# Four RMS norms of a two-layer hybrid block, taken in two halves of the positions beside the weight tiles around them

## The reference

```
for l in range(2):
    h  = rms_norm(x, ln1) * (1 + sc1) + sh1          # layer 0 and 1, 768 positions
    x  = x + g1 * merge(mixers(h @ w_in)) @ w_out
    h2 = rms_norm(x, ln2) * (1 + sc2) + sh2          # 768 positions in layer 0, 512 in layer 1
    x  = x + g2 * square(relu(h2 @ w_mlp1)) @ w_mlp2
return rms_norm(x, final_norm)                       # 512 positions
rms_norm(x, g) = x * rsqrt(mean(x*x over the 1024 channels) + 1e-6) * g
```

## Time and profile before

| | us |
|---|---|
| median of 3 runs | 2155.12 (2152.6 to 2156.09) |
| profiled execution, its own time | 2153.41 |
| its span, first to last instruction | 2151.5 |
| PE busy | 2101.2 (98%) |
| DVE / ACT / POOL busy | 1302.1 / 512.4 / 906.7 |

### The profile page before, as it was taken

How to read it: one execution, slowest core, us unless ns; L and a number is a source line. 1 busy time by engine, 2 the same in 40 slices (tenths; PEclk the granted TensorE clock), 3 DMA queues, 4 the chain that set the end, 5 groups by cost and what they waited for, 6 DMA issues and landing times.

```text
span 2151.5 us, 29928 instructions
## 1 busy us (share of the span) xinstructions
PE 2101.2 (98%) x12112; PEld 1885.5 (88%) x12112; DVE 1302.1 (61%) x1987; ACT 512.4 (24%) x818; POOL 906.7 (42%) x492
## 2 busy tenths in 40 slices
PE   6999999999999999999999999999999999999998
PEld 5999999867899899999999989888777787888886
DVE  6998991555663577576686643693266757263353
ACT  4115121454301230111201112312365213010010
POOL 2531442200244264444434443545511465766662
PEclk9999999999999999999999999999999999999999
DMA  7373355232552134435355326345310532322221
GB/s 286 105 154 101 111 180 155 101 121 101 223 179 79 40 127 144 138 137 177 127 172 169 134 95 189 118 178 170 130 34 24 213 114 70 112 92 95 98 98 69
DMA packets 107980, 277.20 MB, mean 129 GB/s; under 512 B 22938, under 2 KB 42778, under 8 KB 106062
## 3 DMA queue, kind: packets, MB, share of 16 engines
q1 hardware_dynamic: 71520, 200.31, 27.5%
q10 hardware_dynamic: 36334, 75.07, 10.6%
HBM read 237.00 MB, written 37.88 MB: 128 GB/s over the span
## 4 chain that ended last, share of the span: by engine, by line
PE 94%; DVE 3%; ACT 1%; DMA 1%; issue 0%; SPq 0%; POOL 0%; DVEq 0%; ACTq 0%; POOLq 0%
PE ps L497 72%; PE ps L506 3%; PE ps L1135 3%; PE ps L1009 2%; PE ps L1149 2%; PE ps L1185 2%; PE ps L512 1%; PE ps L1035 1%; PE ps L1047 1%; PE ps L614 1%; PE ps L1082 1%; PE ps L860 1%; PE ps L998 1%; DMA raw<-in_w_main 1%; PE ps L737 1%; PE ps L1050 0%
## 5 line engine op out<-in xcount | busy, mean ns | idle before, releaser
L1375 POOL TENSOR_SCALAR whi<-raw 128x1024 fp32r<-128x1024 f32 x244 | 273.6, 1121 | 1192.9 <-PE ps L497 660.7
L1378 POOL TENSOR_TENSOR wlo<-raw,whi 128x1024 fp32r<-128x1024 f32 x244 | 633.6, 2597 | 20.4
L497 PE MATMUL ps<-hh,whi 128*128 128x384 f32 (+1 forms) x1512 | 450.1, 353 | 0.3 <-ACT mr L1814 0.3
L497 PE MATMUL ps<-hl,whi 128*128 128x384 f32 (+1 forms) x1512 | 447.6, 351 | 0.0
L497 PE MATMUL ps<-hh,wlo 128*128 128x384 f32 (+1 forms) x1512 | 447.6, 351 | 0.0
L497 PEld LDWEIGHTS ps<-hh,whi 128*128 128x128 f32 x1512 | 275.3, 188 | 20.2 <-issue 1.1
L497 PEld LDWEIGHTS ps<-hl,whi 128*128 128x128 f32 x1512 | 276.4, 188 | 18.5 <-issue 0.2
L497 PEld LDWEIGHTS ps<-hh,wlo 128*128 128x128 f32 x1512 | 276.3, 188 | 18.6
L2237 DVE SCALAR_TENSOR_TENSOR x<-ps,ada,x 128x384 f32<-128x384 f32 (+1 forms) x160 | 80.4, 546 | 274.8 <-PE ps L497 274.8
L497 PE MATMUL ps<-midh,whi 128*128 128x384 f32 (+1 forms) x768 | 231.1, 354 | 1.8 <-DVE midl L2264 1.8
L497 PE MATMUL ps<-midh,wlo 128*128 128x384 f32 (+1 forms) x768 | 229.6, 353 | 0.0
(11 more groups left out here) (270 smaller groups left out, 3037.1 us busy)
## 6 DMA issues: line engine op xcount, KB each, us to landing
raw<-in_w_main SPq DMA_DIRECT2D x244, 512.0 KB, 3.3
dot_w<-in_ada_dot SPq DMA_DIRECT2D x64, 512.0 KB, 4.1
ada_mixer<-in_ada_w SPq DMA_DIRECT2D x32, 512.0 KB, 4.0
g_d<-gt ACTq DMA_DIRECT2D x24, 384.0 KB, 2.4
gl<-g_d ACTq DMA_DIRECT2D x8, 1152.0 KB, 5.4
ada_first<-in_ada_w SPq DMA_DIRECT2D x16, 512.0 KB, 14.8
cout_d<-cz SPq DMA_DIRECT2D x12, 512.0 KB, 4.9
cout<-cout_d ACTq DMA_DIRECT2D x6, 1024.0 KB, 8.5
```

The lines of the kernel that those rows point to most:

```text
L497: ins = pe.matmul(bank(p, h, a, b), ww[:, w % W_SLOTS, kw * P:(kw + 1) * P], xx[:, kx, a:b], start=(first and i == 0 and j == 0), stop=(la ...
L1375: pool.tensor_scalar(whi[:, u, :], raw[:, u % 2, :], 1.0, 0.0, ALU.mult, ALU.add).then_inc(w_split.sem, 1)
L1378: pool.tensor_tensor(wlo[:, u, :], raw[:, u % 2, :], whi[:, u, :].bitcast(F32), ALU.subtract).then_inc(w_split.sem, 1)
```

## The change

For norms A, B, C and D the last four tiles of the product ahead (`FULL = 4`) are taken half by half: first all four for the first half of the positions (h = 0), then all four for the second (h = 1). Each half result has a PSUM bank of its own (`END_BANKS`). The sums of half 0 stand on PE behind the first tile of the second pass, its spread behind the second. The three start tiles then run eight steps for h = 0 and eight for h = 1; sums and spread of half 1 stand behind steps 2 and 4 of the first eight. For D, which has no product behind it, they stand at the end.

The core of the diff, PE:

```
+        def pe_end(pe, key, n, w, xh, xl):
+            for h in range(2):
+                a, b = h * (n // 2), (h + 1) * (n // 2)
+                for k in range(FULL, KD):
+                    t = w + k - FULL
+                    if h == 0:
+                        wait_w(pe, t)
+                    if (h, k) == (0, FULL):
+                        pe.wait_ge(x_add.sem, x_add.at(added(key, FULL - 2)))
+                    elif (h, k) == (0, KD - 1) or (h, k) == (1, FULL):
+                        pe.wait_ge(x_add.sem, x_add.at(added(key, FULL - 1)))
+                    elif h and k >= FULL + 2:
+                        pe.wait_ge(x_add.sem, x_add.at(added(key, k - 2, 0)))
+                    for i in range(KD):
+                        for j, (ww, xx) in enumerate(((whi, xh), (whi, xl), (wlo, xh))):
+                            ins = pe.matmul(end_bank(key, n, k, h), ww[...], xx[:, i, a:b], ...)
+                    (ins then marks w_used if h, else half_done)
+                    if h and k == FULL:
+                        pe_sums(pe, key, n, 0)
+                    if h and k == FULL + 1:
+                        pe_spread(pe, key, n, 0)
+        def pe_start(pe, key, n, w):
+            pe.wait_ge(x_add.sem, x_add.at(added(key, KD - 2, 1)))
+            for h in range(2):
+                for k in range(KD):
+                    pe.wait_ge(hi_ready.sem, hi_ready.at((*key, k, h)))
+                    ... (whi, wlo) x hh[:, k, a:b] of tiles w, w+1, w+2; wait_w at h == 0, k == 0
+                    pe.wait_ge(lo_ready.sem, lo_ready.at((*key, k, h)))
+                    ... whi x hl[:, k, a:b]
+                    if h == 0 and k == SUMS_AT:      # 2
+                        pe_sums(pe, key, n, 1)
+                    if h == 0 and k == SPREAD_AT:    # 4
+                        pe_spread(pe, key, n, 1)
             if l == 0:
                 pe.wait_ge(ada_ready.sem, ada_ready.at("dots"))
                 pe.wait_ge(prep_act.sem, prep_act.at((1, "v", S5_PARTS - 1)))
-            pe_norm(pe, (l + 1, 1), n)
+            pe_end(pe, (l + 1, 1), n, base + QUARTERS * 16 - 4, midh, midl)
```

DVE, in this order (ACT's follows it: squares of half 0, square of tile 4's half 1, root 0, then the hh of half 0 with the squares of tiles 6 and 7 between):

```
+        def dve_end(dve, key, n, w):
+            for k in range(FULL, KD):
+                residual_half(dve, key, n, k, 0, w)
+                add_squares(dve, key, k - 1, n, None if k == FULL else 0)
+            add_squares(dve, key, KD - 1, n, 0)
+            residual_half(dve, key, n, FULL, 1, w)
+            invert(dve, key, n, 0)
+            add_squares(dve, key, FULL, n, 1)
+            residual_half(dve, key, n, FULL + 1, 1, w)
+            for k in range(KD):
+                if k == 2: add_squares(dve, key, FULL + 1, n, 1)
+                if k == 4: residual_half(dve, key, n, KD - 2, 1, w)
+                if k == 7: residual_half(dve, key, n, KD - 1, 1, w)
+                normalised(dve, key, n, k, 0)            # nt of k, then hl of k - 1
+            add_squares(dve, key, KD - 2, n, 1)
+            low_half(dve, key, n, KD - 1, 0)
+            add_squares(dve, key, KD - 1, n, 1)
+            invert(dve, key, n, 1)
+            for k in range(KD):
+                normalised(dve, key, n, k, 1)
+            low_half(dve, key, n, KD - 1, 1)
```

More of the change, by code:

```diff
@@ L537, in wait_w, with half_spans @@
             pe.wait_ge(w_split.sem, 2 * (t + 1))
[L539 to L554, removed]
+        def half_spans(n):
+            m = n // 2
+            return ((0, 0, m, 0),), (((1, m, LAT, 0), (1, LAT, n, 1)) if n > LAT else ((1, m, n, 0),))
@@ new lines, in norm_bank, with pe_sums @@
+        def norm_bank(n, h):
+            return ps[:, 3, 512 * h:512 * h + n // 2]
+        def pe_sums(pe, key, n, h):
+            pe.wait_ge(sq_used.sem, sq_used.at((key, KD - 1, h)))
+            for b in range(n // (2 * P)):
+                c = h * (n // 2) + b * P
+                ins = pe.matmul(norm_bank(n, h)[:, 2 * b:2 * b + 2], sqa[:, c:c + P], ones[:, 0:2],
+                                start=True, stop=True, skip_group_check=True)
+            ins.then_inc(sq_summed.sem, sq_summed.mark((key, h)))
@@ L940, in pe_layer @@
             else:
-                for k in range(KD):
-                    first_tiles(range(3), k)
+                pe_start(pe, (1, 1), TOK, t0)
                 tile(3, 3)
@@ L1219, in pe_layer @@
                         ins.then_inc(w_used.sem, w_used.mark(w + m))
[L1220 to L1226, removed]
+            wait_w(pe, w + 3)
+            pe.wait_ge(x_add.sem, x_add.at((l, 0)))
+            product(pe, 0, w + 3, full, mh, ml, n, True, True).then_inc(w_used.sem, w_used.mark(w + 3))
+            pe_end(pe, (l, 2), n, w + FULL, mh, ml)
             base = t0 + MLP
-            early = 3
-            for t in range(QUARTERS * 16):
+            pe_start(pe, (l, 2), n, base)
+            for t in range(3, QUARTERS * 16 - 4):
                 q, m = divmod(t, 16)
@@ L1239, in pe_layer @@
                 wait_w(pe, base + t)
[L1240 to L1250, removed]
+                if m < KD:
                     product(pe, p, base + t, full, hh, hl, n, True, True).then_inc(
@@ L1413, in act_norm @@
[L1413 to L1426, removed]
+                act.wait_ge(sq_used.sem, sq_used.at((key, max(k - 2, 1)) if h is None or k < FULL + 2 else (key, k - 2, h)))
@@ new lines, in act_norm @@
+        def act_norm(act, key, n):
+            last = key == (DEPTH, 1)
+            for k in range(FULL):
+                act_square(act, key, n, k)
+            for k in range(FULL, KD):
+                act_square(act, key, n, k, 0)
+            act_square(act, key, n, FULL, 1)
+            act_root(act, key, n, 0)
+            act_square(act, key, n, FULL + 1, 1)
+            for k in range(KD):
+                if k == 4:
+                    act_square(act, key, n, KD - 2, 1)
+                if k == 7:
+                    act_square(act, key, n, KD - 1, 1)
+                if not last:
+                    act_hi_half(act, key, n, k, 0)
+            act_root(act, key, n, 1)
+            if not last:
+                for k in range(KD):
+                    act_hi_half(act, key, n, k, 1)
@@ L1879, in invert @@
[L1879 to L1889 removed]
+            act_norm(act, (DEPTH, 1), LAT)
```

255 lines of the change are left out of this document (168 added, 87 removed).

## The result

The changed kernel takes 2159.19 us (median of 7 runs, 2157.84 to 2162.72) against 2155.12 for the one before (7 runs, 2152.12 to 2156.74): a ratio of 1.0025, 95% interval [1.0013, 1.0036]. The interval leaves out 1, so it is slower, by about 0.25%. Its profiled execution has a span of 2157.4 us against 2151.5, 5.9 more.

The account below looks back on a forecast made before the run. PE, busy 98% of the span, bounds the kernel, with about 49.5 us exposed at the norms. Norms 4.5 - 0.3 - 1.1 + 1.6 = 4.7 us faster, clock 6.8 slower: net 2.1 slower, 2157 us, range 2143 to 2165.

Parts of the forecast that it names:

- The likeliest case: Port contention at the norms, a new dots wait and clock falls behind waits: 2.1 us slower, 2157; chance 0.45.
- the wait for the dots: Before layer 1, PE stands idle 4.8 us ahead of tile 60, whose bank pair holds the dot products.
- the clock: Gaps inside full products drop PE to half clock: four falls of 1.7 us, 6.8 in all.
- the store of x: Store to HBM before layer 1 comes some 5 us later on ACT: costs 0, far end 2.
- A, B, C, D if all hides: Norms before layer 0's MLP, layer 1, layer 1's MLP, and at the end: gains 10.0, 10.0, 6.65, 1.6 us.
- waits at A: Norm before layer 0's MLP: PE waits 1.3 us for tile six's residual, 4.2 for half 1's sums; 5.5 together.
- waits at B: Norm before layer 1: 5.5 us as at the first norm, plus 4.8 for the dots.
- waits at C: Norm before layer 1's MLP: 0.8 diagonal, 3.0 start product, 3.7 half 1's sums, 0.2 last end tile; 7.7 us.
- the sign "2.7 us and more": POOL's weight splits beside DVE's work at the norms would take 2.7 us and more if the forecast were right.
- Rival 2: Port contention at the norms is small: 22.5 us gained, 2132.6, or half of it, 2144; chance 0.13.
- Rival 1: Clock stays up through gaps of 4 us surrounded by full work: 4.7 us faster, 2150.4; chance 0.22.
- Rival 3: POOL wins the port each time, start products wait 5 us: 8.6 us beyond the forecast, 2165.7; chance 0.18.

Follow-up runs that it names:

- the last kernel: Changed kernel with other dots banks, later half 1 sums, earlier store of x, late load of the fourth tile, earlier residual of tile 62: 2131.51 us, ratio 0.9899.
- the later sums: Changed kernel with the sums of half 1 behind four steps of the start product, not two, and the spread behind five, not four: 2150.64 us, ratio 0.9972.
- the third experiment: Changed kernel with hl reading the norm's PSUM bank, not hh, so one SBUF input and a wrong low part: 2143.75 us, ratio 0.9941.
- fourth split out of the way: Changed kernel with the load of tile w + 3 waiting until the squares of half 1 have been read: 2153.84 us, ratio 0.9995.
- three edits: Changed kernel with other bank pairs before attention, later sums and spread of half 1, and the early store of x: 2139.52 us, ratio 0.9921.
- four edits: Changed kernel with other bank pairs before attention, later half 1 sums, early store of x, and late load of the fourth tile: 2136.75 us, ratio 0.9916.
- the other banks: Changed kernel with tile 60's half in a free bank pair before attention, the dots awaited ahead of tile 62: 2154.35 us, ratio 0.9996.

## Why the prediction was right

The forecast was 2157.0, 2.1 us slower; measured were 4.1 by the medians and 5.9 by the spans. The likeliest case was the one that came: contention, the wait for the dots, and falls of the clock behind the waits. That the sum came so close is in part luck: by the spans PE waited 4.7 us less than forecast and the clock cost 4.3 more, which nearly cancels, and the gains were 2.3 too high and the store of x 1.8 too low. Its terms in us (gain positive), against the traces; "all hidden" is measured with the last kernel's stretches at A and B (at C, with the later sums: 47.91 less its five waits, 4.46), and the clock's price is what is left of a stretch when that and the waits are taken off.

| term | predicted | measured |
|---|---|---|
| A, B, C, D if all hides | 10.0, 10.0, 6.65, 1.6 | 9.5, 10.0, 5.2, 1.2 |
| waits at A | 5.5 | 0.87 + 3.11 = 4.0 |
| waits at B | 5.5 + 4.8 | 4.58 + 0.88 + 3.12 = 8.6 |
| waits at C | 7.7 | 0.75 + 0.75 + 1.71 + 2.99 = 6.2 |
| clock | 6.8 | 2.1 + 6.4 + 2.6 = 11.1 |
| store of x | 0 (far end 2) | 1.8 |
| other stretches | 0 | 0.2 |
| net | -2.1 | 26.0 - 18.8 - 11.1 - 1.8 - 0.2 = -5.9 |

*Gains if hidden:* right to half a microsecond at A and B (at A the last kernel still has 0.61 us of idle time, 61.10 busy of 61.71, as the changed one has beside its two waits); B shows it exactly, since 70.93 - 60.89 = 10.04. At C it was 1.4 too high. The pace of 256 columns isn't the reason: nine matmuls of a half step take 1.08 us, 0.12 each, so the pair costs the 13 ns that I took. The rest lies in sums, spreads and the first matmuls behind a wait, 3.1 and not 1.7; I did not separate them.

*Contention:* right in mechanism, 5.3 us lost by four low parts at A and 0.4 by the diagonal against 6.5 laid out. I had given the additions a share too; at A and B they ran at 0.55 behind the spread, and only at C, beside a split, one took 1.25 where another took 0.41. The splits of A took 2.40 to 2.79, so of the sign "2.7 us and more" one in four came true. PE waited 0.87 and 3.11 for 1.3 and 4.2. The Trainium skill, page "SBUF — State Buffer", section "Who interferes with whom", has the rule that I weighed, a lock for a whole instruction where DVE reads two SBUF inputs; the third experiment agrees with it (0.61 with one, up to 2.15 with two). Rival 2, small contention, falls: its 2132.6 was reached only with all five edits. Its sum also left out the fall of the clock behind the dots, which doesn't depend on contention.

*The dots:* 4.58 for 4.8, in its place.

*The clock:* the term that was mis-sized. I counted four falls at the price of the earlier trace rows. There were four, but they cost 2.1 at A, 2.6 behind the dots, 3.8 behind B's sums (6.4 less 2.6) and 2.6 at C: behind each of them the clock stayed low for longer than the first start step had shown. Rival 1 falls: the stands of 3.0 to 4.6 us inside full products lowered the clock each time. Its one support falls too: the gap of 1.85 us that kept clock 1.00 in the earlier trace rows is followed by a fall in four of the other kernels. And my theory that every wait has a fall behind it was too strong, see the last section.

*The store:* mis-sized too, a term that I had put at 0. I had looked at the next use, thirty microseconds on, and not at what stands behind the store on ScalarE: the round trip of `zs` through DRAM, whose `us` PE reads at 1358. The store started 5.0 us ahead of the start product's end where it had 10.9 before.

*Rival 3* (POOL wins the port each time): DVE got in between `whi` and `wlo`. The low part of 717.98 ended at 719.38, behind the `whi` split that ended at 718.97 and inside the `wlo` split that followed, which took 2.57 and not 2.40. The waits at the start product were 0.87, 0.88 and 1.71 and not 5, so it falls. The chance of slower adds up to 0.29 by its own parts (0.18, 0.02 and a fifth of 0.45), not 0.27.

## What to carry to other kernels

Work put "beside" a product is hidden only if the engine that does it keeps its bare pace there. So first ask which engine the finer order wakes up: here the earlier release of weight slots started POOL's splits just when DVE needed the port. Then place the one instruction of the bounding engine that waits as late as its result allows: two constants, a bank table with its wait and one earlier store turned 0.25% slower into 0.8% faster, with all the rest of the change as it was. And a wait of TensorE is priced with its echo in the clock, 6.4 us on top of 8.6 at B.

## What the runs showed beside

**The same stand, another price.** From the sums to the spread of half 1 there are the same 25 matmuls at A and B. Behind a wait of 1.60 us (fourth split out of the way) they ran once at full clock and once not:

```profile
729.87:733.78 3.91, 3.91 (x25) 3.91 (x25) 0.75 (x2) 0.27 (x1) 0.45 (x1) 1.00 0.74 267
1291.06:1296.53 5.47, 5.47 (x25) 5.47 (x26) 0.75 (x2) 0.27 (x1) 1.85 (x2) 0.69 0.51 192
```

Behind 3.1 us it took 5.48 at A, and at B 6.98 in the changed kernel, 5.51 and 5.34 with the dots' wait gone or filled. So one stand costs 0, 1.5 or 3 us by clock. What decides it these runs don't show; without the dots' wait, some 45 us earlier, it was 1.5 less at B.

The gap of the earlier trace rows, 1.83 to 1.85 us in every kernel, some 170 us ahead of norm B, says the same. The same 5 us behind it hold 54 matmuls at clock 1.00 before the change and in six of the other kernels, and 45 at 0.66 in four (later sums, low part, three edits, four edits), none of which touches this place. The changed kernel, then the one with later sums:

```profile
1077.57:1082.57 5.00, 5.00 (x54) 4.54 (x55) 4.69 (x7) 0.36 (x1) 3.39 (x2) 1.00 0.32 108
1075.30:1080.30 5.00, 5.00 (x45) 3.90 (x46) 4.37 (x7) 0.36 (x1) 3.08 (x2) 0.66 0.31 107
```

A single trace can't price a stand; I took one price from one trace.

**DVE and POOL in lockstep.** Behind C, DVE's `ms` and `midl` and POOL's splits pass the port to and fro, 4.3 us a round. With the other banks this went on until PE needed `midl`, and it stood 2.20 us; so it did with the later sums. In the changed kernel POOL had once waited 0.59 us for a transfer, DVE got in with 0.68 and 1.42 at the place of 1.53 and 2.77, and PE waited for nothing. The changed kernel, then the one with other banks:

```profile
1825.11 0.68 DVE L2410 TENSOR_TENSOR ms<-mr 128x512 f32<-128x512 f32 x1
1825.83 1.42 DVE L2414 TENSOR_TENSOR midl<-ms,midh 128x512 fp32r<-128x512 f32 x1
...
1825.23 1.47 POOL L1432 TENSOR_SCALAR whi<-raw 128x1024 fp32r<-128x1024 f32 x1 [0.59 <-DMA raw<-in_w_main]
```

```profile
1826.15 1.52 DVE L2412 TENSOR_TENSOR ms<-mr 128x512 f32<-128x512 f32 x1
1827.71 2.77 DVE L2416 TENSOR_TENSOR midl<-ms,midh 128x512 fp32r<-128x512 f32 x1
```

So 2 us of a 5 us gain can be lost hundreds of matmuls on, at a place that the edit doesn't touch. I take it for chance of the phase between two engines, which no run varied alone; the last two kernels don't have this wait, the one with three edits does.
